# Two conv-FFN up-projections as Strassen block products inside a two-block transformer kernel

## The chip, the cores and the metric

One core of one Trainium2 chip runs the whole kernel in one launch. The metric is device time in microseconds (us). Engines are named as in the profile: PE is TensorE (PEld its weight loads), DVE VectorE, ACT ScalarE, POOL GpSimd, SP SyncE, which issues weight loads from DRAM.

## What is computed

Two transformer blocks follow each other on 1024 tokens of 1024 channels (the second adds 16 meta tokens). Each ends with a projection of the mixer's output, a residual with two norms, and a convolutional feed-forward part. In both blocks this tail is, cut to what matters here:

```python
y = mixed @ w_out                                  # 1024 x 1024
x = x + gate * rmsnorm(y)                          # gate is 1 in the second block
h = modulate(rmsnorm(x))                           # no shift in the second block
u = dwconv(h @ w_up, conv) + bias                  # w_up: 1024 x 5632, three taps over tokens
val, g = split(u)                                  # 2816 each
out = (val * silu(g)) @ w_down                     # gelu in the second block
x = x + gate2 * rmsnorm(out)
```

All is float32. A product of float32 matrices is made of three matmuls of rounded parts: high weights on high data, low weights on high data, high weights on low data.

## The kernel before

Data lie transposed: channels on the 128 partitions, tokens along the free axis. `mixer_out_to_ffn` (L3223) builds, for either block, the instruction streams of all five engines from w_out to the gate product; `both_mixers` (L3635) strings the first block's, its down-projection (`DownToMerge`, L2405, which goes on with the second block's input projections), the second block's and its down-projection (`DownToOutput`, L2979) together on each engine.

The streams go by steps. Steps 0 to 15 are w_out: two parts of the tokens (448 and 576 in the first block, 460 and 580 in the second), eight tiles of 128 output channels each. The steps after are up tiles of 128 of the 5632 channels; tile j belongs to pair j // 2, the gate tile when j is even and the value tile when it is odd, 22 pairs. The first FIRST = 11 tiles are done on part 0 of the tokens first and on part 1 later (L3241), the other 33 at once. One step is 8 groups of 128 input channels, for each group three matmuls per piece of columns (L3376 to L3378): 512 columns in the first block (`PIECES1`), 342 in the second.

- SP loads a step's weights, 512 KB, into one of two raw buffers (L3291), once their last user's low part is done.
- ACT rounds them to the high part one step ahead (`weight_high`, L3267), waits for the step's matmuls, copies PSUM to a row buffer (L3453, L3459), multiplies by the middle tap and adds the bias (L3467, the centring), and applies silu or gelu to the gate tile (L3472).
- DVE subtracts the high part from the raw weights (`weight_low`, L3277), adds the two outer taps (L3576) and forms the gate product into `g` in SBUF (L3581), 22 rows of 1024 tokens.
- While PE works at the next steps, the norms of a part run in a chain of eight steps (`chain_of`, L3246): squares, means, a spread of the reciprocals by matmul (L3333), residual (L3499, L3504), stores of x by POOL, second norm, scaling (L3511), rounding to `h_hi` and `h_lo`. The sums of squares are matmuls of one column (L3316, L3323) put between the step's own. Part 1's chain ends before step 27, where the first tile needs it.

The down-projection (`Down`, L2114) takes the tokens in four parts of 256; each of its steps is one of the 22 rows of `g` and one 512 KB weight tile, in three buffers. ACT and DVE split the weights and the 256 columns of `g` two steps ahead (L2201, L2215), PE runs 24 matmuls of 256 columns (L2351 to L2353). Norms and residual of the last part run beside it; POOL loads their x rows (L2329). The rows y, x and the squares of a part lie in `g` itself, in columns that are done with (L2146).

## Time and profile before

| | us |
|---|---|
| median of 3 runs | 3636.86 (3633.42 to 3645.36) |
| profiled execution, from its first to its last instruction (its span) | 3639.3 |
| PE busy in it | 3469.9 |
| DVE busy | 2010.0 |
| ACT busy | 1552.9 |
| POOL busy | 140.0 |

The profile is of one execution on the chip. No time is given for what lies around its span; the span is 0.07% above the median and inside the runs' own range, so it is read as that execution's time. Busy times are of instructions on the engine; matmuls are pipelined, each shown longer than the distance to the next, so PE's rate is read from where tiles start, not from durations. The granted TensorE clock is full over most of the span (mean 0.973).

### The profile page before, as it was taken

The numbers are of one execution on the slowest core, as the hardware profiler recorded it, in microseconds if no ns is written. First come the engines' busy times: TensorE is split into PE (matmuls) and PEld (weight loads), VectorE is DVE, ScalarE is ACT, GpSimd is POOL, SyncE is SP. The second block draws the span as 40 slices with busy tenths as digits, with TensorE's granted clock in tenths as the row PEclk, the third lists the DMA queues.
The fourth block names the chain that finished last, engine by engine and source line by source line (L and its number), as shares of the span: only waits on it lengthen the run. The fifth ranks groups of instructions, "written<-read, shape, count | busy, mean of one in ns | idle before, by whom it ended". The sixth has DMA issues, their size and how long they took to land.

```text
span 3639.3 us, 71215 instructions
## 1 busy us (share of the span) xinstructions
PE 3469.9 (95%) x30719; PEld 3187.7 (88%) x30719; DVE 2010.0 (55%) x3131; ACT 1552.9 (43%) x2539; POOL 140.0 (4%) x267
## 2 busy tenths in 40 slices
PE   7999899999889979999999999999999999999999
PEld 4787779888877878888888999899999899999999
DVE  5477767787757745543335785232224653333676
ACT  4556654444337734433334654111114443333554
POOL 2000000000000001000000111000001000000000
PEclk9999999999989989999999999999999999999999
DMA  6233443223233124211113665111114421111665
GB/s 243 75 129 130 147 171 104 90 82 115 76 70 71 26 80 133 89 58 47 47 47 121 209 215 161 30 33 44 47 47 125 131 71 47 47 47 54 200 214 165
DMA packets 321840, 367.30 MB, mean 101 GB/s; under 512 B 14803, under 2 KB 261046, under 8 KB 321528
## 3 DMA queue, kind: packets, MB, share of 16 engines
q1 hardware_dynamic: 304424, 309.64, 27.3%
q0 software_dynamic: 17104, 53.11, 4.4%
q8 instruction: 243, 3.98, 0.4%
q14 instruction: 69, 0.57, 0.0%
HBM read 302.79 MB, written 59.90 MB: 100 GB/s over the span
## 4 chain that ended last, share of the span: by engine, by line
PE 57%; DVE 3%; ACT 2%; issue 1%; DVEq 0%; DMA 0%; POOL 0%; ACTq 0%
PE psum L3376 10%; PE psum L3378 10%; PE psum L3377 10%; PE psum L2351 4%; PE psum L2826 4%; PE psum L2827 4%; PE psum L2828 4%; PE psum L2353 4%; PE psum L2352 4%; PE psum L2688 1%; DVE u_val L3576 1%; DVE w_lo L3277 1%; PE psum L3323 1%; ACT u_val L3467 0%; DVE g L3581 0%
## 5 line engine op out<-in xcount | busy, mean ns | idle before, releaser
L3376 PE MATMUL psum<-mix_h_hi,w_hi 128*128 128x342 f32 (+5 forms) x1848 | 636.3, 344 | 17.1 <-DVE w_lo L3277 15.2
L3377 PE MATMUL psum<-mix_h_hi,w_lo 128*128 128x342 f32 (+5 forms) x1848 | 632.3, 342 | 0.0
L3378 PE MATMUL psum<-mix_h_lo,w_hi 128*128 128x342 f32 (+5 forms) x1848 | 631.9, 342 | 0.0
L2218 DVE TENSOR_TENSOR w_lo<-w_raw,w_hi 128x1024 fp32r<-128x1024 f32 (+1 forms) x167 | 195.9, 1173 | 398.4 <-ACT w_hi L2208 396.9
L3376 PEld LDWEIGHTS psum<-mix_h_hi,w_hi 128*128 128x128 f32 x1848 | 349.0, 189 | 47.5 <-DVE w_lo L3277 18.6
L2208 ACT ACTIVATE w_hi<-w_raw 128x1024 fp32r<-128x1024 f32 (+1 forms) x167 | 170.3, 1020 | 491.3 <-PE psum L2828 325.3
L3378 PEld LDWEIGHTS psum<-mix_h_lo,w_hi 128*128 128x128 f32 x1848 | 348.9, 189 | 26.8
L3377 PEld LDWEIGHTS psum<-mix_h_hi,w_lo 128*128 128x128 f32 x1848 | 349.2, 189 | 26.3
L3453 ACT ACTIVATE xs<-psum 128x1024 f32<-128x1024 f32 (+1 forms) x66 | 67.9, 1029 | 486.2 <-PE psum L3378 486.2
L2351 PE MATMUL psum<-down_ghi,w_hi 128*128 128x256 f32 x944 | 269.8, 286 | 0.6 <-DVE down_glo L2223 0.3
L2353 PE MATMUL psum<-down_glo,w_hi 128*128 128x256 f32 x944 | 266.9, 283 | 0.0
L2352 PE MATMUL psum<-down_ghi,w_lo 128*128 128x256 f32 x944 | 266.9, 283 | 0.0
L3277 DVE TENSOR_TENSOR w_lo<-w_raw,w_hi 128x1024 fp32r<-128x1024 f32 x142 | 173.4, 1221 | 154.7 <-ACT w_hi L3273 154.4
L2826 PE MATMUL psum<-h_hi,w_hi 128*128 128x348 f32 (+2 forms) x736 | 238.3, 324 | 0.5 <-DVE h_lo L2515 0.5
L2827 PE MATMUL psum<-h_hi,w_lo 128*128 128x348 f32 (+2 forms) x736 | 237.2, 322 | 0.0
L2828 PE MATMUL psum<-h_lo,w_hi 128*128 128x348 f32 (+2 forms) x736 | 236.9, 322 | 0.0
L3576 DVE SCALAR_TENSOR_TENSOR u_val<-xs,prm,u_val 128x1024 f32<-128x1024 f32 x68 | 87.4, 1285 | 247.8 <-ACT u_val L3467 245.3
L757 PE MATMUL psum<-h_hi,w_hi 128*128 128x512 f32 (+1 forms) x536 | 209.0, 390 | 0.7 <-DVE w_lo L923 0.7
L758 PE MATMUL psum<-h_hi,w_lo 128*128 128x512 f32 (+1 forms) x536 | 199.6, 372 | 0.0
L759 PE MATMUL psum<-h_lo,w_hi 128*128 128x512 f32 (+1 forms) x536 | 199.4, 372 | 0.0
L3576 DVE SCALAR_TENSOR_TENSOR u_gate<-xs,prm,u_gate 128x1024 f32<-128x1024 f32 x64 | 82.2, 1285 | 200.1 <-ACT u_gate L3467 197.7
L2351 PEld LDWEIGHTS psum<-down_ghi,w_hi 128*128 128x128 f32 x944 | 180.3, 191 | 1.9 <-DVE down_glo L2223 1.6
(490 smaller groups left out, 7999.1 us busy)
## 6 DMA issues: line engine op xcount, KB each, us to landing
w_raw<-in_w_down SPq DMA_DIRECT2D x118, 512.0 KB, 4.1
w_raw<-in_w_up SPq DMA_DIRECT2D x110, 512.0 KB, 3.7
w_raw<-in_w_in SPq DMA_DIRECT2D x59, 512.0 KB, 4.0
down_w_raw<-in_w_down SPq DMA_DIRECT2D x58, 512.0 KB, 3.9
rw_operands<-step_set SPq DMA_DIRECT2D x16, 1024.0 KB, 6.3
mod_w<-in_w_mod POOLq DMA_DIRECT2D x32, 512.0 KB, 6.1
w_raw<-in_w_out SPq DMA_DIRECT2D x32, 512.0 KB, 3.6
unit<-rw_operands SPq DMA_DIRECT2D x22, 512.0 KB, 5.0
```

The lines of the kernel that those rows point to most:

```text
L757: mm(out, k.w_hi[:, s, w], k.h_hi[:, kk, x], start=(kk == 0), stop=False)
L2351: nc.tensor.matmul(out, w_hi[:, w], g_hi[:, :], start=(n == 0 and c % 2 == 0), stop=False, skip_group_check=True)
L2352: nc.tensor.matmul(out, w_lo[:, w], g_hi[:, :], start=False, stop=False, skip_group_check=True)
L2353: last = nc.tensor.matmul(out, w_hi[:, w], g_lo[:, :], start=False, stop=(n == KF - 1), skip_group_check=True)
L2826: nc.tensor.matmul(out, w_hi[:, w], x_hi[:, xk, x], start=(kk == 0), stop=False)
L2827: nc.tensor.matmul(out, w_lo[:, w], x_hi[:, xk, x], start=False, stop=False)
L2828: last = nc.tensor.matmul(out, w_hi[:, w], x_lo[:, xk, x], start=False, stop=end)
L3277: nc.vector.tensor_tensor(k.w_lo[:, slot(i), :], k.w_raw[:, slot(i), :], k.w_hi[:, slot(i), :].bitcast(F32), ALU.subtract).then_inc(w_low, 1)
L3376: nc.tensor.matmul(out, k.w_hi[:, s, w], xh[:, kk, x], start=(kk == 0), stop=False)
L3377: nc.tensor.matmul(out, k.w_lo[:, s, w], xh[:, kk, x], start=False, stop=False)
L3378: last = nc.tensor.matmul(out, k.w_hi[:, s, w], xl[:, kk, x], start=False, stop=(kk == KD - 1))
L3576: last = nc.vector.scalar_tensor_tensor(out=u[:, :], in0=x[:, left + q:left + q + SEQ], scalar=tap[q], in1=u[:, :], op0=ALU.mult, op1=ALU.add)
```

## The change

An up pair becomes one 2 x 2 x 2 block product in the Strassen-Winograd form. Its blocks: of the weights, value (row 1) and gate (row 2) tiles, each in two halves of 4 x 128 input channels; of h, the same two halves of channels and two halves of the tokens. The seven products are called P1 to P7; P1 and P2 need only half 0 of the tokens. Four operands are sums of blocks of h (`t1` to `t4`, made once, with `b22` copied), four are sums of weight blocks (made for each pair). Each product is 4 groups of three matmuls on n columns: n is 512 in the first block, 516 (two banks of 258) in the second, where 1032 tokens from the 8th on are taken.

The step list (`plan_steps`): 32 half steps of w_out on halves of 512 (516) tokens; 16 early steps, P1 and P2 of the pairs 3, 5, 7, 9, 0, 1, 11, 13; then the late steps of pairs 0 to 21, P6, P7, P5, P4, P3 for the early pairs and P1, P6, P7, P5, P2, P4, P3 for the others. From pair 1 to 14 early and fresh pairs alternate. The weights of a step are split three steps ahead into a ring of four buffers, raw tiles lie in four. P1 is copied by ACT to the value row before P2 is added to it; the other five products are taken by DVE (`take`), with adds and subtracts that put the output rows together. The gate product goes to DRAM, `Down` reads it back in parts of 256 columns through POOL's queue. Chains take sixteen half steps. The core of the diff:

```diff
-FIRST = 11
+EARLY = [3, 5, 7, 9, 0, 1, 11, 13]
...
-    jobs = [(j, (0,)) for j in range(FIRST)] + [(j, (1,)) for j in range(FIRST)] + \
-           [(j, (0, 1)) for j in range(FIRST, TILES_UP)]
+def plan_steps(banks):
+
+    steps = [("O", u, h) for u in range(2 * KD) for h in range(2)]
+    if banks == 1:
+        early = [("P1", EARLY[0])]
+        for last, i in zip(EARLY, EARLY[1:]):
+            early += [("P1", i), ("P2", last)]
+        early.append(("P2", EARLY[-1]))
+    else:
+        early = [(kind, i) for i in EARLY for kind in ("P1", "P2")]
+    late = [(kind, i) for i in range(KF)
+            for kind in (("P6", "P7", "P5", "P4", "P3") if i in EARLY else ("P1", "P6", "P7", "P5", "P2", "P4", "P3"))]
+    return steps + early + late
...
+    def weight_low(dve, s):
+        src, r = source(s)
+        dve.wait_ge(*w_high.at(s + 1))
+        nc.vector.tensor_tensor(ring[s % 4][:, 1, :], src, ring[s % 4][:, 0, :].bitcast(F32), ALU.subtract).then_inc(w_low.sem, 1)
+        if s + 1 < STEPS and s + 1 >= first_late:
+            kind, i = steps[s + 1]
+            if kind == "P6":
+                add_weights(dve, i)
+            elif kind == "P4":
...
+    def add_weights(dve, i):
...
+        dve.drain()
+        nc.vector.tensor_tensor(tmp[0][:, :], g[:, 0:512], g[:, 512:1024], ALU.add).then_inc(w_added.sem, 1)
+        dve.drain()
+        nc.vector.tensor_tensor(g[:, 0:512], g[:, 0:512], v[:, 0:512], ALU.add).then_inc(w_added.sem, 1)
+        nc.vector.tensor_tensor(tmp[1][:, :], tmp[0][:, :], v[:, 0:512], ALU.add).then_inc(w_added.sem, 1)
...
     def gpsimd(pool):
...
+        for m in range(KF):
+            pool.wait_ge(*g_ready.at(m + 1))
+            pool.dma_start(k.g_dram[m], uv[:, :]).then_inc(g_stored.sem, 16)
+            if m >= FIRST_ROWS:
+                pool.wait_ge(*g_stored.at(16 * m))
+                after.load_first(pool, 0 if m == FIRST_ROWS else m - 1, m)
...
     def tensor(pe):
...
+            elif kind == "P4":
+                pe.wait_ge(*took.at(5 * i + 2))
+            elif kind == "P3":
+                pe.wait_ge(*took.at(5 * i + 3))
...
+        for s in range(STEPS):
+            kind, i = steps[s][0:2]
+            pe.wait_ge(*w_low.at(s + 1))
+            bank_free(s)
...
     def scalar(act):
...
+        def centre_gate(i):
+            act.wait_ge(*took.at(5 * i + 4))
...
+        def centre_val(i):
+            act.wait_ge(*took.at(5 * i + 5))
...
+        for s in range(STEPS):
+            kind, i = steps[s][0:2]
+            if s + 3 < STEPS:
+                weight_high(act, s + 3)
...
+            if s >= first_late and i and s == late_at[i]:
+                activate(i - 1)
+            if kind == "O":
+                if steps[s][2]:
+                    act.wait_ge(*acc_done.at(s + 1))
+                    keep_unit(i)
+            elif kind == "P1":
+                keep_p1(s)
+            elif kind == "P2":
+                keep_c11(s)
+            elif kind == "P4":
+                centre_gate(i)
+            elif kind == "P3":
+                centre_val(i)
...
     def vector(dve):
...
+        def add_turns(kk):
...
+            tt(f["t1"], h0[0][kk][:, :].bitcast(F32), b12, ALU.subtract)
+            tt(f["t3"], b12, b22_row, ALU.subtract)
+            dve.drain()
+            tt(f["t1"], f["t1"], h0[1][kk][:, :].bitcast(F32), ALU.add)
+            dve.drain()
+            tt(f["t2"], b22_row, f["t1"], ALU.add).then_inc(t_added.sem, 1)
+            dve.drain()
+            tt(f["t4"], h0[0][kk + 4][:, :].bitcast(F32), f["t2"], ALU.subtract)
+            dve.drain()
+            tt(f["t4"], f["t4"], h0[1][kk + 4][:, :].bitcast(F32), ALU.add).then_inc(t4_added.sem, 1)
...
+            elif e == 14:
+                scale_rows(a, 4)
+                if a == 0:
+                    low_rows(0)
+                else:
+                    add_turns(0)
+            elif e == 15:
+                if a == 0:
+                    low_rows(4)
+                else:
+                    for kk in range(1, 4):
+                        add_turns(kk)
+                    for which in TURNS[0:3]:
+                        low_turns(which)
...
+            if at == 1 and i:
+                val_tap(i - 1, 2)
+            elif at == 2 and i:
+                product(i - 1)
+            if s + 3 < STEPS:
+                weight_low(dve, s + 3)
+            elif s + 3 < STEPS + 2:
+                after.split(dve, s + 3 - STEPS)
+            if at == 0 and i:
+                val_tap(i - 1, 0)
+            elif kind == "P3":
+                gate_taps(i)
...
+            if s in (first_late, first_late + 1):
+                low_turns(TURNS[3 + s - first_late])
+            if s >= first_late:
+                take(s)
...
+    def load_part(self, pool, p):
+        pool.dma_start(self.g_part[p % 2][:, :, :],
+                       self.k.g_dram[:, :, self.cols(p)].rearrange("n p c -> p n c")).then_inc(self.part_landed[p], 16)
...
         for p in range(SEQ // PART):
             pool.wait_ge(self.low, KF * (p + 1))
+            if p + 2 < SEQ // PART:
+                self.load_part(pool, p + 2)
             for kk in range(4):
                 self.load_x(pool, p, kk)
```

`take` waits for the step's matmuls (`acc_done`) and counts `took`, five a pair in the order P6, P7, P5, P4, P3; `at` is the number of steps since the pair's first late one.

## Rows read from the trace of the kernel before

**Rows 1.** The page: busy shares by engine, and the chain that ended last

```profile
PE 3469.9 (95%) x30719; PEld 3187.7 (88%) x30719; DVE 2010.0 (55%) x3131; ACT 1552.9 (43%) x2539; POOL 140.0 (4%) x267
...
PE psum L3376 10%; PE psum L3378 10%; PE psum L3377 10%; PE psum L2351 4%; PE psum L2826 4%; PE psum L2827 4%; PE psum L2828 4%; PE psum L2353 4%; PE psum L2352 4%; PE psum L2688 1%; DVE u_val L3576 1%; DVE w_lo L3277 1%; PE psum L3323 1%; ACT u_val L3467 0%; DVE g L3581 0%
```

**Rows 2.** Timeline of PE: start us, us, engine line op out<-in xcount [idle <-releaser]

```profile
1312.71 0.74 PE L3376 MATMUL psum<-mix_hi,w_hi 128*128 128x448 f32 x1 [11.88 <-DVE w_lo L3277]
...
1949.78 0.28 PE L2351 MATMUL psum<-down_ghi,w_hi 128*128 128x256 f32 x1
...
2734.47 0.37 PE L3376 MATMUL psum<-mix_hi,w_hi 128*128 128x460 f32 x1
...
3361.84 0.28 PE L2351 MATMUL psum<-down_ghi,w_hi 128*128 128x256 f32 x1
```

**Rows 3.** Timeline of ACT, up tiles of the first, then of the second block

```profile
1603.84 1.25 ACT L3467 ACTIVATE u_gate<-xs,prm 128x1024 f32<-128x1024 f32 x1
1605.00 1.05 ACT L3273 ACTIVATE w_hi<-w_raw 128x1024 fp32r<-128x1024 f32 x1
...
1615.04 1.24 ACT L3467 ACTIVATE u_val<-xs,prm 128x1024 f32<-128x1024 f32 x1
...
3327.94 1.03 ACT L3453 ACTIVATE xs<-psum 128x1026 f32<-128x1026 f32 x1 [7.16 <-PE psum L3378]
...
3339.31 1.03 ACT L3453 ACTIVATE xs<-psum 128x1026 f32<-128x1026 f32 x1 [8.11 <-PE psum L3378]
```

**Rows 4.** Timeline of ACT, first block, w_out units of half 0 and half 1

```profile
1324.68 0.55 ACT L3437 ACTIVATE mix_y<-psum 128x448 f32<-128x448 f32 x1 [2.93 <-PE psum L3378]
...
1329.54 0.55 ACT L3437 ACTIVATE mix_y<-psum 128x448 f32<-128x448 f32 x1 [2.92 <-PE psum L3378]
...
1382.25 0.71 ACT L3437 ACTIVATE mix_y<-psum 128x288 f32<-128x288 f32 x2 [0.90 <-PE psum L3378]
...
1390.54 0.71 ACT L3437 ACTIVATE mix_y<-psum 128x288 f32<-128x288 f32 x2 [0.89 <-PE psum L3378]
```

**Rows 5.** Groups by shape on DVE from 1290 us: xcount | busy, mean ns | idle

```profile
L3576 DVE SCALAR_TENSOR_TENSOR u_val<-xs,prm,u_val 128x1024 f32<-128x1024 f32 x68 | 87.4, 1285 | 247.8 <-ACT u_val L3467 245.3
...
L2218 DVE TENSOR_TENSOR w_lo<-w_raw,w_hi 128x512 fp32r<-128x512 f32 x16 | 11.1, 692 | 143.6 <-ACT w_hi L2208 143.6
...
L3499 DVE TENSOR_TENSOR mix_temp<-mix_y,psum 128x576 f32<-128x576 f32 x8 | 5.7, 748 | 0.5 <-PE psum L3337 0.5
```

**Rows 6.** Timeline of DVE, first block, an up tile

```profile
1593.99 2.65 DVE L3576 SCALAR_TENSOR_TENSOR u_val<-xs,prm,u_val 128x1024 f32<-128x1024 f32 x2 [8.88 <-ACT u_val L3467]
1596.71 1.23 DVE L3581 TENSOR_TENSOR g<-u_val,mix_up 128x1024 f32<-128x1024 f32 x1
1597.85 1.22 DVE L3277 TENSOR_TENSOR w_lo<-w_raw,w_hi 128x1024 fp32r<-128x1024 f32 x1
```

**Rows 7.** Groups by shape on ACT from 1290 us

```profile
L2208 ACT ACTIVATE w_hi<-w_raw 128x512 fp32r<-128x512 f32 x16 | 10.1, 632 | 156.7 <-PE psum L2828 156.7
```

**Rows 8.** Timeline of PE, start of the first block's down

```profile
1959.19 0.58 PE L2351 MATMUL psum<-down_ghi,down_w_hi 128*128 128x256 f32 x1 [3.29 <-DVE down_glo L2223]
1959.57 0.41 PE L2352 MATMUL psum<-down_ghi,down_w_lo 128*128 128x256 f32 x1
1959.78 0.41 PE L2353 MATMUL psum<-down_glo,down_w_hi 128*128 128x256 f32 x1
...
1962.12 0.28 PE L2352 MATMUL psum<-down_ghi,down_w_lo 128*128 128x256 f32 x1
1962.24 0.28 PE L2353 MATMUL psum<-down_glo,down_w_hi 128*128 128x256 f32 x1
```

**Rows 9.** A stretch of the first down, and DMA issues: xcount, KB, us to landing

```profile
core 0: us, PE busy (x) PEld busy (x) DVE busy (x) ACT busy (x) POOL busy (x), PEclk, DMA share, GB/s
2000.00:2200.00 200.00, 199.41 (x1674) 198.15 (x1673) 162.79 (x301) 118.30 (x214) 25.79 (x48) 1.00 0.65 211
...
mod_w<-in_w_mod POOLq DMA_DIRECT2D x32, 512.0 KB, 6.1
```

More of the change, by code:

```diff
@@ L2183, in nth @@
     def nth(self, i):
-        return i // 3 + 1 if i < self.TWO else self.TWO // 3 + (i - self.TWO) // 2 + 1
+        return sum(self.slot(j) == self.slot(i) for j in range(i + 1))
     def depth(self, i):
@@ L2917, in vector @@
             elif i + 2 == self.total:
-                self.next.weight_low(dve, 0)
+                for s in range(2):
+                    self.next.weight_low(dve, s)
             if q == 7:
@@ L3206, in vector @@
             self.finish_rows(dve, self.last, half)
-FIRST = 11
+EARLY = [3, 5, 7, 9, 0, 1, 11, 13]
+QUEUE = len(EARLY)
+KEPT = {i: j for j, i in enumerate(EARLY + [i for i in range(KF) if i not in EARLY])}
+X_BUFFER = [6, 7] + [i // 2 - 1 if i % 2 and i < 14 else 6 + i % 2 for i in range(2, KF)]
+FIRST_ROWS = 14
 def half_groups(n):
@@ new lines, in mixer_out_to_ffn @@
+    squared, added, resid, squared2, added2 = (signal(q, t) for q, t in (
+        ("squared", 2 * KD), ("added", 2 * KD - 2), ("residual", 2 * KD), ("squared_again", 2 * KD), ("added_again", 2 * KD)))
+    summed, meaned, rooted, diags, spread = (signal(q, t) for q, t in (
+        ("summed", 2), ("meaned", 4), ("rooted", 4), ("diags", 4), ("spread", 4)))
+    xin_landed = [signal(f"x_landed{s}", 16 * 4) for s in range(4)]
+    x_stored = [signal(f"x_stored{a}", 16 * KD) for a in range(2)]
+    scaled, shifted, high, low = (signal(q, t) for q, t in (
+        ("scaled", 2 * KD), ("shifted", 2 * KD), ("high", KD), ("low", KD)))
@@ L3284, in sync @@
+    def sync(sp):
+        for r in range(TILES):
+            if r >= 4:
+                sp.wait_ge(*w_low.at(released[r - 4]))
+            elif before and r < 2:
+                sp.wait_ge(before.low, before.total - 1 + r)
             elif before:
-                sp.wait_ge(before.low, before.total - 1 + i)
-            if i < UNITS:
-                src = w_out[:, :, unit(i)[1] * P:unit(i)[1] * P + P]
-            else:
-                c = col(job(i)[0])
+                sp.wait_ge(before.merged, KD)
+            if r < UNITS:
+                src = w_out[:, :, r % KD * P:r % KD * P + P]
+            else:
+                if r < UNITS + QUEUE:
+                    c = (EARLY[r - UNITS] + side[1]) * P
+                else:
+                    i, gate = divmod(r - UNITS - QUEUE, 2)
+                    c = (i + side[0 if gate else 1]) * P
@@ new lines, in spreads, with chain @@
+            pe.wait_ge(*diags.at(norm(a, second)))
+            for t, m in half_groups(n):
+                if t == 0:
+                    last = nc.tensor.matmul(spread_out[:, 0:4 * P], k.ones[:, :], dg[:, 0:4, :], start=True, stop=True)
+                elif m < P:
+                    last = nc.tensor.matmul(spread_out[:, t * P:t * P + m], k.ones[0:m, :], dg[0:m, t, 0:m],
+                                            start=True, stop=True)
+            last.then_inc(spread.sem, 1)
+        def chain(a, e, kk):
+            if e == 1 and kk == 1:
+                sums(a)
+            elif e == 2 and kk == 3:
+                spreads(a, 0)
+            elif e == 5 and kk in (0, 2):
+                sum_residual(a, kk // 2)
+            elif 6 <= e <= 10 and kk == 1:
+                sum_residual(a, e - 4)
+            elif e == 10 and kk == 3:
+                sum_residual(a, 7)
+            elif e == 12 and kk == 2:
+                spreads(a, 1)
@@ L3473, in scalar @@
+        activate(KF - 1)
         after.scalar(act)
@@ new lines, in scale_rows @@
+        def scale_rows(a, j0):
+            dve.wait_ge(*spread.at(norm(a, 1)))
+            dve.wait_ge(*x_stored[a].at(16 * KD))
+            dve.drain()
+            for j in range(j0, j0 + 4):
+                row = y[a][:, order[a][j], :]
+                if shift is not None:
+                    nc.vector.tensor_tensor(row, row, spread_out[:, 0:n], ALU.mult).then_inc(scaled.sem, 1)
+                else:
+                    nc.vector.scalar_tensor_tensor(out=row, in0=row, scalar=gain_pre(order[a][j]), in1=spread_out[:, 0:n],
+                                                   op0=ALU.mult, op1=ALU.mult).then_inc(scaled.sem, 1)
@@ L3522, in vector, with val_tap, product @@
+        def val_tap(i, q):
+            dve.wait_ge(*centred_v.at(i + 1))
+            last = tap(i, False, q)
+            if q == 2:
+                last.then_inc(tapped_v.sem, 1)
+        def product(i):
+            dve.wait_ge(*activated.at(i + 1))
+            dve.drain()
+            nc.vector.tensor_tensor(uv[:, :], uv[:, :], ug[:, :], ALU.mult).then_inc(g_ready.sem, 1)
         spec["prepare"]()
@@ L3525, in vector @@
         if not before:
-            weight_low(dve, 0)
-        for i in range(STEPS):
-            if before and i < 4:
-                for kk in (2 * i, 2 * i + 1):
-                    before.merged_low(dve, 1, kk)
-            if i + 1 < STEPS and (i or not before):
-                weight_low(dve, i + 1)
-            elif i:
-                after.split(dve, 0)
-            if 1 <= i <= UNITS and (i - 1) % KD:
-                a, n = unit(i - 1)
-                m = hs[a]["n"]
+            for s in range(3):
+                weight_low(dve, s)
```

848 lines of the change are left out of this document (503 added, 345 removed).

## The prediction, made before the changed kernel had run

> **What bounds the kernel now.** I read the page's busy shares first, then the chain that ended last: TensorE (PE) is busy 95% of the span and most of that chain is PE, with the three matmul lines of the function that changes at its head, 10% each [rows 1]. So the up-projections are on the path, and fewer columns through PE is time, as long as PE stays the one that ends last. The timeline of PE gives the two stretches that change: first block, w_out and up, from 1312.7 to the first down matmul at 1949.8, 637 us; second block 2734.5 to 3361.8, 627 us [rows 2]. In the timeline of ScalarE (ACT) one up tile follows the other every 11.20 us (48 matmuls of 512 columns, 0.233 us each) and, in the second block, every 11.37 us (72 of 342, 0.158 us) [rows 3]. In that rhythm VectorE (DVE) has 8.88 us of idle ahead of a tile [rows 6], so before the change neither DVE nor ACT matters.
>
> **What PE saves.** A pair (gate tile and value tile) needs 8 block products before and 7 after, 12 matmuls each. First block: 22 x (22.40 - 7 x 2.80) = 62 us. In the second block a product is 24 matmuls of 258 columns: a 256-column one is 0.12 us after the other [rows 8], so 2.88 us a product, and 22 x (22.73 - 20.16) = 57 us; with the slope between 342 and 512 columns it would be 2.89. Together 119 us.
> The Trainium skill (TensorE: Matmul & The Clock Gate, Back-to-back issue gap) puts isolated matmuls at columns / 2.4 plus 2.5 ns, 216 ns at 512 and 110 ns at 258. By it the change would save another 37 us in the second block; the row at 512 shows 233 instead, so the trace doesn't bear that out, and I take the rows.
>
> **What DVE and ACT get.** Durations for 512 elements: weight split L on DVE 0.69 us [rows 5]; two DVE instructions without a drain between them start 0.08 us before the other's end, with a drain 0.08 after it [rows 6]. So L fills 0.61; a drained sum S, or a product taken from PSUM T (0.75 at 576, so 0.68 at 512 [rows 5]), fills 0.76; a 1024 tap V is 1.285 + 0.08 = 1.36, the gate product R 1.23 + 0.08 = 1.31 [rows 5, 6]. A pair before cost DVE 2 splits of 1024, 4 V, R. Now it has 7 L (5 with its P1 and P2 done early), 4 sums, 5 T, 4 V, R: 17.7 us fresh, 15.7 early, against 19.6 and 14.0 on PE. An early pair alone overruns; an early and a fresh one make 34.2 (one sum more in front of an early pair) against 33.6.
> Then the order within the engines. ACT's step begins with the next weights' high part; the centring (1.15 us from its start to the next instruction's [rows 3]) stands at the end of steps P4 and P3, and waits for DVE's T. DVE's next step begins with L, which waits for that high part, which is queued on ACT behind the centring. So twice per pair DVE stands still for about 0.1 + 1.15 + 0.6 (a 512 high part takes 0.63 [rows 7]) + 0.1 = 1.9 us, with nothing to put there. DVE's list of steps, from one P3 taken to the next (W is the 1.9; of three sums in a row the last fills 0.61). Early pair: P6 W+L+V+T 4.63, P7 V+L+T 2.73, P5 R+L+3S+T 4.81, P4 L+T 1.37, P3 W+L+2V+T 5.99, together 19.5 us. Fresh pair before an early one: P1 W+L+V 3.87, P6 V+L+S+T 3.49, P7 R+L+T 2.68, P5 L+3S+T 3.50, P2 L 0.61, P4 L+T 1.37, P3 W+L+S+2V+T 6.75, together 22.3; fresh before fresh one S less, 21.5. PE can't run away from it: P4 waits for T of P7, P3 for T of P5, and its weights are made three steps ahead. PE's waits are then 8.2 us in an early-fresh couple and 1.9 in a fresh pair.
> Pairs 1 to 21: 7 early x 19.5 + 6 x 22.3 + 8 x 21.5 = 442 us in the first block, 444 in the second (516 elements), against 372 and 383 on PE.
>
> **The entry to the late steps** (counted from PE's start of step 45, the last third but one of the early products). Half 1 of y must be scaled, shifted, turned into four sums of operands and rounded. DVE: scaling and two splits to 8.7; four rows of six drained sums, 4.4 each, to 27.7; three groups of four lows to 35.2; then L, four lows, T to 39.4; L, three weight sums, four lows, T of P7 to 45.4. P6 also waits for the eighth early pair, kept on ACT behind three groups of rounding, 31.8. P4 starts at 45.4, P3 ends at 51.0, where eight steps of 2.80 would end at 22.4: 28.6 us lost, 27.5 in the second block. Before, eleven first-half tiles hid this. T of P3 ends at 55.9; so PE's last P3 ends at 55.9 + 442 - 7.2 (its lead over T) = 491 from step 45; second block 492.
>
> **The rest.** w_out, half 0: 8 x 5.60 + 2.2 for the low clock at the start, as before, 47.0 (before 8 x 4.86 [rows 4]). Half 1: a unit took 8.29 us with two sums of squares between its 48 matmuls of 288 [rows 4], which by the slope from the 256 ones are 0.134 each, 6.4; so 0.95 for one such insertion, and 11 of them make 8 x 5.60 + 10.5 = 55.3 (in the second block five groups of columns for four, 1.06 each). At steps 32 and 33 PE waits for the low rows of half 0 and then for the last square: 6.8 us, plus 3 at a lower clock; 3.4 and 2 in the second block. 13 early steps 36.4 + 10.5 = 46.9. **First block** 47.0 + 55.3 + 9.8 + 46.9 + 491 = 650, before 637: +13. **Second block** 47.2 + 57.8 + 5.4 + 49.1 + 492 = 652, before 627: +25. **Into down**: the first two down steps start at once; the third needs DVE, which ends its last product 7 us behind PE: PE waits 8.5 us where it waits 3.29 now [rows 8]: +5 twice. The gate products now go through DRAM. The store is hidden: 512 KB land in about 6 us [rows 9], and the next centring of the value comes 9.7 us after. Reading back, 2.9 MB a part on POOL's queue and ahead of the residual's x rows, meets weights at 211 GB/s and a DMA share of 0.65 [rows 9]: between 0 and 24 us; there is a third of the engines free, so I take 5. PSUM banks, the three-step weight lead and the four raw tiles cost nothing: their waits lie inside those above (without that cover the tightest is a bank's, P3 waiting for T of P5, 1.7 us in a couple). The halves of 512 + 512 tokens in place of 448 + 576 leave the attention's last copies the same elements in fewer instructions: under 1 us of gain, taken as none.
> Sum: +13 + 25 + 10 + 5 = +53 on the profiled execution's span of 3639.3, which is 2.4 above the median of 3636.9: **3690 us** (3689.9). Its own range, with 3% on DVE's slots (27 us), 0.2 us on each wait (17) and 10 on the entry: 3650 to 3730.
>
> **Rivals.**
> **Faster: DVE's standstill behind ACT doesn't take place**, because the answer is there before L asks. Then couples run at 34.2, fresh pairs at PE's 19.6, and the 133 us of the two late stretches over PE's time shrink to about 10. Entry costs stay. First block 586, second 595, down +5: 3639 - 51 - 32 + 5 = 3561, or 3559 against the median. Between the ends it decides by the length of the standstill: at 1.1 us instead of 1.9 the kernel breaks even. For it: 8.88 us of idle DVE, and engines that in this trace answer each other in 0.1 us. Against: the order in the code is fixed. 24%, with all that lies between.
> **Slower: the part loads hold the weights up.** Six loads of 2.9 MB, each with some 8 weight tiles under way; if the two share evenly a tile lands in over 4 us where PE eats one in 2.87, and after the slack of two tiles PE waits about 4 us a load: +24 on the forecast, 3714. For it: share 0.65. Against: it is not 1.
> The Trainium skill (DMA: Bandwidth & Descriptors, Queues, rings and completion order) says that each DMA engine serves its queues in turn, packet by packet. By that rule the loads take from the weights instead of waiting behind them.
> **Slower: the clock.** After a wait of 3.29 us PE's 256-column matmuls lay 0.21 apart, not 0.12, for nearly 3 us [rows 8], the lower level of 1.2 GHz. The wait before P4 of an early pair is 4.9 us. If four steps of each couple ran there, 33.6 + 11 is 44.8 and PE is slower than DVE: +3 a couple, 40 in all 14 early pairs, 3730. For one or two steps it hides behind DVE.
> These two 14% together. The change does do what it says: 154 steps of 12 matmuls of 512 are 7/8 of the columns.
>
> **How the numbers follow.** DVE-bound with standstill 62%; faster rival 24%; the slower two 14%. About 0.3% (11 us) is what a measurement can tell from no change: 6% for that, taken from the first two cases' edges. Slower 0.70, same 0.06, faster 0.24. The range leaves out the lower part of the fast rival and the far end of the slow ones: 3600 to 3740.
>
> **What would show it.** PE's idle up by about 170 us, its releasers DVE's takes (P7, P5) and w_lo; a gap of some 20 us in PE before the first P6 of each block; DVE near 85% busy in the late stretch, with idle of 1.9 us ended by ACT's w_hi twice a pair; couples 42 us apart, fresh pairs 21.5. Wrong if couples come at 34 us, if DVE's idle there is under 1 us a pair, if PE's waits in down end on DMA, or if the entry gap is short.

## The result and the profile after

The changed kernel takes **3720.8 us** (median of 4 runs, 3717.3 to 3728.6) where the kernel before takes 3639.7 (4 runs): ratio 1.0224, 95% interval 1.0205 to 1.0244. That is slower, by 81 us; forecast were 53. First the page of the profiled execution (its span 3722.4 us): busy times, and the chain that ended last by engine.

```profile
PE 3406.6 (92%) x30711; PEld 3081.6 (83%) x30711; DVE 2404.7 (65%) x3809; ACT 1582.8 (43%) x2735; POOL 182.5 (5%) x335
...
PE 38%; DVE 14%; issue 4%; DVEq 3%; ACT 3%; DMA 2%; ACTq 0%; POOL 0%
...
g_scratch<-mix_u_val POOLq DMA_DIRECT2D x44, 512.0 KB, 4.0
down_g_part<-g_scratch POOLq DMA_DIRECT2D x6, 2816.0 KB, 17.2
```

PE is busy 63 us less than before and yet the span is 83 longer [rows 1]: PE stands idle 316 us instead of 169, and DVE works 395 us more. (The forecast saving for PE was 119 us at full clock. The mean granted clock is 0.957 where it was 0.973, and how much of the difference that makes was not traced.) The timeline of PE, at the starts of the stages:

```profile
1307.49 0.79 PE L3586 MATMUL psum<-mix_hi,mix_w_split 128*128 128x512 f32 x1 [9.67 <-DVE mix_w_split L3407]
...
1495.80 0.77 PE L3586 MATMUL psum<-mix_t_hi,mix_w_split 128*128 128x512 f32 x1 [23.76 <-ACT mix_x_val L3680]
...
1970.42 0.28 PE L2369 MATMUL psum<-down_ghi,down_w_hi 128*128 128x256 f32 x1
...
2763.65 0.28 PE L3586 MATMUL psum<-mix_hi,mix_w_split 128*128 128x258 f32 x1
...
3431.66 0.28 PE L2369 MATMUL psum<-down_ghi,down_w_hi 128*128 128x256 f32 x1
```

| stage, from such starts | before | after | difference | forecast |
|---|---|---|---|---|
| ahead of the first block | 1312.7 | 1307.5 | -5 | 0 |
| first block | 637.1 | 662.9 | +26 | +13 |
| its down and what follows, to the second block | 784.7 | 793.2 | +9 | +7.5 |
| second block | 627.4 | 668.0 | +41 | +25 |
| its down, to the end | 277.4 | 290.8 | +13 | +7.5 |

Each block has the 24 us gap ahead of its first P6. The rest is in the late steps. Here are PE's waits in the changed kernel over the whole run (engine, line, what it waited for: us in total, times, longest):

```profile
PE psum L3586 <- DVE mix_x_gate L3858: 86.2, 34, 5.7
PE psum L3586 <- ACT mix_x_val L3680: 46.3, 2, 23.8
PE psum L3586 <- DVE mix_w_split L3407: 19.4, 29, 9.7
...
PE psum L2369 <- DVE down_glo L2240: 12.2, 6, 5.1
```

L3858 is DVE's take of P7, for which P4 waits. Why DVE is late with it, where it had 8.88 us of idle ahead of a tile before [rows 6], shows in its own timeline, one fresh pair of the first block from one P4 taken to the next:

```profile
1835.21 0.69 DVE L3862 TENSOR_TENSOR mix_x_gate<-mix_u,psum 128x512 f32<-128x512 f32 x1
1837.73 0.69 DVE L3407 TENSOR_TENSOR mix_w_split<-mix_w_raw,mix_w_split 128x512 fp32r<-128x512 f32 x1 [1.83 <-ACT mix_w_split L3402]
1838.52 2.64 DVE L3870 SCALAR_TENSOR_TENSOR mix_u_gate<-mix_x_gate,prm,mix_u_gate 128x1024 f32<-128x1024 f32 x2
1841.25 0.69 DVE L3864 TENSOR_TENSOR mix_x_val<-psum,mix_u 128x512 f32<-128x512 f32 x1
1843.78 0.69 DVE L3407 TENSOR_TENSOR mix_w_split<-mix_w_sum,mix_w_split 128x512 fp32r<-128x512 f32 x1 [1.83 <-ACT mix_w_split L3402]
1844.56 2.64 DVE L3870 SCALAR_TENSOR_TENSOR mix_u_val<-mix_x_val,prm,mix_u_val 128x1024 f32<-128x1024 f32 x2
...
1855.55 0.69 DVE L3426 TENSOR_TENSOR mix_w_sum<-mix_w_sum,mix_w_raw 128x512 f32<-128x512 f32 x1
1856.93 0.69 DVE L3407 TENSOR_TENSOR mix_w_split<-mix_w_sum,mix_w_split 128x512 fp32r<-128x512 f32 x1 [0.70 <-ACT mix_w_split L3402]
1857.71 0.69 DVE L3862 TENSOR_TENSOR mix_x_gate<-mix_u,psum 128x512 f32<-128x512 f32 x1
```

And ACT over the first two of those takes:

```profile
1835.94 1.25 ACT L3687 ACTIVATE mix_u_gate<-mix_x_gate,prm 128x1024 f32<-128x1024 f32 x1 [1.54 <-DVE mix_x_gate L3862]
1837.09 0.61 ACT L3402 ACTIVATE mix_w_split<-mix_w_raw 128x512 fp32r<-128x512 f32 x1
1841.98 1.25 ACT L3696 ACTIVATE mix_u_val<-mix_x_val,prm 128x1024 f32<-128x1024 f32 x1 [4.28 <-DVE mix_x_val L3864]
1843.13 0.61 ACT L3402 ACTIVATE mix_w_split<-mix_w_sum 128x512 fp32r<-128x512 f32 x1
```

DVE takes P4 (ends 1835.90). ACT's centring starts at 1835.94, the next weights' rounding, queued behind it, at 1837.09, and DVE's split at 1837.73: 1.83 us idle, the standstill forecast at 1.9. The same follows the take of P3. A third one, 0.70 us, was not forecast: the last of three weight sums (L3426) has to be rounded by ACT before DVE can split it, and DVE has nothing to do in between.

### The profile page after: what moved, and what is told of

The parts are those of the page before. It is cut to its first block, busy times and chain, and to the rows that moved or that the text cites. A ratio compares the mean times of both kernels' runs of the same rounds, so it can differ in the third digit from the quotient of the medians.

```text
span 3722.4 us, 73022 instructions
## 1 busy us (share of the span) xinstructions
PE 3406.6 (92%) x30711; PEld 3081.6 (83%) x30711; DVE 2404.7 (65%) x3809; ACT 1582.8 (43%) x2735; POOL 182.5 (5%) x335
## 4 chain that ended last, share of the span: by engine, by line
PE 38%; DVE 14%; issue 4%; DVEq 3%; ACT 3%; DMA 2%; ACTq 0%; POOL 0%
PE psum L3586 5%; PE psum L3588 4%; PE psum L3587 4%; PE psum L2846 4%; PE psum L2847 4%; PE psum L2848 4%; PE psum L2369 3%; PE psum L2371 3%; PE psum L2370 3%; DVE mix_u_val L3870 3%; DVE mix_u_gate L3870 2%; DMA down_w_raw<-in_w_down 2%; DVE mix_w_split L3407 2%; ACT mix_w_split L3402 2%; PE psum L2705 1%
## 5 line engine op out<-in xcount | busy, mean ns | idle before, releaser
L2235 DVE TENSOR_TENSOR down_w_lo<-down_w_raw,down_w_hi 128x1024 fp32r<-128x1024 f32 x228 | 270.5, 1186 | 442.2 <-ACT down_w_hi L2209 440.1
L3586 PE MATMUL psum<-mix_t_hi,mix_w_split 128*128 128x258 f32 (+1 forms) x1056 | 358.2, 339 | 145.6 <-DVE mix_x_gate L3858 86.2
L2369 PE MATMUL psum<-down_ghi,down_w_hi 128*128 128x256 f32 x1408 | 404.5, 287 | 12.4 <-DVE down_glo L2240 12.2
L2371 PE MATMUL psum<-down_glo,down_w_hi 128*128 128x256 f32 x1408 | 399.7, 284 | 0.0
L2370 PE MATMUL psum<-down_ghi,down_w_lo 128*128 128x256 f32 x1408 | 399.5, 284 | 0.0
L3586 PEld LDWEIGHTS psum<-mix_t_hi,mix_w_split 128*128 128x128 f32 x1056 | 211.0, 200 | 180.7 <-DVE mix_w_split L3407 106.1
L3587 PE MATMUL psum<-mix_t_hi,mix_w_split 128*128 128x258 f32 (+1 forms) x1056 | 351.2, 333 | 0.0
L3588 PE MATMUL psum<-mix_t_lo,mix_w_split 128*128 128x258 f32 (+1 forms) x1056 | 350.8, 332 | 0.0
L2369 PEld LDWEIGHTS psum<-down_ghi,down_w_hi 128*128 128x128 f32 x1408 | 271.6, 193 | 14.5 <-DVE down_glo L2240 14.1
L2370 PEld LDWEIGHTS psum<-down_ghi,down_w_lo 128*128 128x128 f32 x1408 | 271.8, 193 | 0.3
L2371 PEld LDWEIGHTS psum<-down_glo,down_w_hi 128*128 128x128 f32 x1408 | 271.5, 193 | 0.0
L3587 PEld LDWEIGHTS psum<-mix_t_hi,mix_w_split 128*128 128x128 f32 x1056 | 211.3, 200 | 15.9
## 6 DMA issues: line engine op xcount, KB each, us to landing
down_g_part<-g_scratch POOLq DMA_DIRECT2D x6, 2816.0 KB, 17.2
```

The source lines that it names most:

```text
L2235: last = self.nc.vector.tensor_tensor(self.lo[s][:, 0:w], self.raw[s][:, 0:w], self.hi[s][:, 0:w].bitcast(F32), ALU.subtract)
L2369: nc.tensor.matmul(out, w_hi[:, w], g_hi[:, :], start=(n == 0 and c % 2 == 0), stop=False, skip_group_check=True)
L2370: nc.tensor.matmul(out, w_lo[:, w], g_hi[:, :], start=False, stop=False, skip_group_check=True)
L2371: last = nc.tensor.matmul(out, w_hi[:, w], g_lo[:, :], start=False, stop=(n == KF - 1), skip_group_check=True)
L3586: nc.tensor.matmul(out, w[:, 0, c], xh[:, x], start=(first and kk == 0), stop=False, skip_group_check=True)
L3587: nc.tensor.matmul(out, w[:, 1, c], xh[:, x], start=False, stop=False, skip_group_check=True)
```

## The experiments

All times below are medians beside runs of the kernel before on the same chip. The experiments ran on four chips, on which the kernel before takes 3636.9 to 3644.4 us, so small differences between two of these kernels are better read from their ratios than from their microseconds. The stage times come from one profiled execution of each. "Late steps" are the time from ACT's first to its last centring of a value in a block, a couple is an early and a fresh pair (mean over the first 14 intervals). The last column has the usual distance between the P3s of two fresh pairs at the end of a block, on PE.

| kernel | us | ratio to before (95%) | late steps, 1st / 2nd block | couple | fresh pair |
|---|---|---|---|---|---|
| changed kernel | 3720.8 | 1.0205 to 1.0244 | 454.3 / 454.8 | 42.8 | 22.5 |
| rounding ahead of centring | 3619.6 | 0.9928 to 0.9963 | 401.9 / 404.0 | 37.6 | 19.6 to 20.0 / 20.1 |
| sum order | 3720.6 | 1.0189 to 1.0241 | 447.5 / 448.7 | 42.3 | 21.9 |
| both | 3619.2 | 0.9917 to 0.9964 | 400.5 / 404.0 | 37.6 | 19.6 / 20.1 |
| both, takes first | 3621.7 | 0.9918 to 0.9952 | 403.6 / 404.5 | 37.6 | 20.1 / 20.2 |
| first, sums on GpSimd | 3636.2 | 0.9976 to 0.9995 | 401.5 / 403.2 | 37.8 | 19.6 / 20.1 |

**Is it the standstill?** The rounding for the next step goes ahead of the centring in ACT's queue:

```diff
+            elif kind in ("P4", "P3"):
+                if s + 4 < STEPS:
+                    weight_high(act, s + 4)
+                if kind == "P4":
+                    centre_gate(i)
+                else:
+                    centre_val(i)
```


> On ScalarE the rounding of the weights of the step after the next three stands ahead of the centring in the steps P4 and P3, and nothing else changes. Theory (VectorE stands still behind ScalarE's centring, 1.83 us of idle twice a pair): both idles go, a pair costs VectorE 3.8 us less. A couple of an early and a fresh pair goes from 43.2 to 35.6 us, two fresh pairs lie 19.6 us apart in the first block and 20.2 in the second, where TensorE itself ends last. Late steps 455 us -> 382 and 385; the whole kernel 3721 - 144 = 3577 us. Rival (the standstill only stands in front of other work that is late anyway, a product's release or a drain): VectorE's idle moves to other lines and couples stay above 40 us: 3690 or more. In between, if one of the two standstills was real: about 3650.

The kernel takes 101 us less and is 0.5% faster than the kernel before, from the order of two instructions. Both 1.83 us idles are gone and fresh pairs go at PE's pace. So the theory holds, and the rival with couples above 40 falls. But the expectation was 144 us: couples stop at 37.6 where it had 35.6. In this kernel's DVE timeline the split no longer waits, and a tap does:

```profile
1837.61 0.68 DVE L3407 TENSOR_TENSOR mix_w_split<-mix_w_sum,mix_w_split 128x512 fp32r<-128x512 f32 x1
1839.07 2.65 DVE L3875 SCALAR_TENSOR_TENSOR mix_u_val<-mix_x_val,prm,mix_u_val 128x1024 f32<-128x1024 f32 x2 [0.78 <-ACT mix_u_val L3696]
```

The taps read what ACT centres, and three of a couple's four centrings make DVE wait 0.78 us, 2.3 us a couple. One wait of 0.3 for a rounding is left. DVE's filled time is 34.4 (32.4 busy, 2.0 of short gaps and drains). Together that is 37.1, which three of the first block's seven couples take. The others take 0.3 to 1.6 us more, mostly because DVE waits 0.3 to 1.0 for PE's product, and so the mean is 37.6. So the 3.1 us of waits for centring in the expectation of the GpSimd run below are 0.8 too high.

**The third wait.** The sum that P6 needs is made second:

```diff
-    SUM = {"P5": 1, "P7": 2, "P6": 3, "P3": 4}
+    SUM = {"P5": 1, "P6": 2, "P7": 3, "P3": 4}
```


> Of the three weight sums of a pair the one that P6 needs is made second instead of third; ScalarE rounds it while VectorE makes the last one. Theory: the idle of 0.70 us ahead of P6's weight split, once a pair, falls to about 0.1; VectorE sets the pace, so 42 pairs x 0.6 = 25 us less, 3696 us, with couples at 42.0 and fresh pairs at 21.9 us. Rival (that wait is hidden in front of a later one): 3721, the two standstills behind the centring grow by what this one gives.

Fresh pairs come down to the 21.9 expected, couples only by 0.4, the late steps by 7 and 6 us: half of what was expected. In couples that wait is 0.4 us in the changed kernel, not 0.7. The median shows nothing of it: in this kernel's profile the same code ahead of the first block took 11 us longer (see the last section). So the median is inconclusive, and the timeline shows a term that is real but smaller.

> The edits of the two kernels before together. Theory: couples of 35.6 - 1.2 = 34.4 us, close to TensorE's 33.6, fresh pairs at TensorE's 19.6 and 20.2: another 16 us below the first alone, 3561 us. Rival (the waits are in one chain, so that the second edit gives nothing once the first is made): 3577, no more than the first edit alone.

The time is the same as with the first edit alone: with the two standstills gone PE sets the pace of fresh pairs, and the third wait is covered. The rival is right.

**Order or sum of DVE's work?** What is left in couples is 37.6 against PE's 33.6.

```diff
+            if s >= first_late and s + 4 < STEPS and steps[s + 4][0] == "P6":
+                add_weights(dve, steps[s + 4][1])
+            if at == 0 and i:
+                val_tap(i - 1, 0)
+            elif at == 1 and i:
+                val_tap(i - 1, 2)
+            elif at == 2 and i:
+                product(i - 1)
```


> On top of the two edits together (rounding ahead of centring, sum order; 3619 us): in each step VectorE takes the product before the taps and the gate product of the pair before, and makes the three weight sums behind the take. The early pairs there still take 17.3 us against TensorE's 14.0, with TensorE waiting 1.3 us before P4 for the take of P7 and 1.8 before P3 for that of P5, and VectorE standing 0.79 us before a tap for the centring. Theory (what is left is the order of VectorE's work in the early pairs): couples go from 36.9 to about 34.6 us, 7 couples in each of two blocks, 32 us: 3587 us. Rival (VectorE's sum of work over a couple, not its order, sets 36.9): 3619 us, the waits only move to P3's take.

Early pairs fall from 17.3 to 16.7 us, the fresh ones between them rise from 20.1 to 20.8 in the second block, and the sum stays. The rival is right: a couple is DVE's filled time and its waits for ACT, in whatever order.

**Work taken off DVE.** The four weight sums of a pair go to GpSimd (`nc.gpsimd.tensor_tensor` in place of `nc.vector.tensor_tensor`, in the loop over the gate products, with waits for the splits that read the same buffers).

> On top of the first edit (rounding ahead of centring; 3620 us), the four weight sums of a pair are made by GpSimd instead of VectorE. VectorE is busy 32.3 us of a couple's 37.6 there, with 2.0 of drains and 3.1 us of waits for centring. Theory (VectorE's sum of work sets the couples): 8 sums of 0.76 us less a couple, the couples come down to TensorE's 33.6, 7 x 3.6 us in each of two blocks: 3570 us. Rival (the sums on GpSimd and VectorE's instructions on two operands in SBUF hinder each other, so that one engine's time is added to the other's): VectorE's splits and taps get longer than 0.69 and 1.28 us and the couples stay at 37 us or more: 3620 us or above.

Groups by shape over a stretch of the first block's late steps, of the kernel with both edits first (1570 to 1900 us), then of this one on DVE (1590 to 1916 us), then its sums on GpSimd over the whole run (xcount | busy, mean ns):

```profile
L3875 DVE SCALAR_TENSOR_TENSOR mix_u_gate<-mix_x_gate,prm,mix_u_gate 128x1024 f32<-128x1024 f32 x34 | 43.7, 1285 | 10.6 <-ACT mix_u_gate L3687 8.9
L3407 DVE TENSOR_TENSOR mix_w_split<-mix_w_raw,mix_w_split 128x512 fp32r<-128x512 f32 x59 | 40.5, 686 | 1.3 <-ACT mix_w_split L3402 1.3
...
L3869 DVE TENSOR_TENSOR mix_x_val<-psum,mix_u 128x512 f32<-128x512 f32 x17 | 11.8, 693 | 1.6
```

```profile
L3884 DVE SCALAR_TENSOR_TENSOR mix_u_gate<-mix_x_gate,prm,mix_u_gate 128x1024 f32<-128x1024 f32 x34 | 55.3, 1626 | 10.7 <-ACT mix_u_gate L3696 8.6 <-issue 0.4
L3407 DVE TENSOR_TENSOR mix_w_split<-mix_w_raw,mix_w_split 128x512 fp32r<-128x512 f32 x58 | 50.8, 876 | 1.8 <-ACT mix_w_split L3402 1.8
...
L3878 DVE TENSOR_TENSOR mix_x_val<-psum,mix_u 128x512 f32<-128x512 f32 x17 | 11.8, 693 | 1.6
```

```profile
L3417 POOL TENSOR_TENSOR mix_w_raw<-mix_w_raw,mix_w_raw 128x512 f32<-128x512 f32 x44 | 88.3, 2007 | 17.0 <-issue 17.0
...
L3420 POOL TENSOR_TENSOR mix_w_sum<-mix_w_sum,mix_w_raw 128x512 f32<-128x512 f32 x44 | 57.3, 1302 | 271.8 <-DVE mix_w_split L3407 271.8
```

The rival is right. A sum costs GpSimd 1.30 us on one line and 2.01 on another, which runs beside DVE's taps for 63 of its 88 us. The gate tile's taps on DVE go from 1285 to 1626 ns, the splits of raw weights from 686 to 876. Within this one run, taps that no GpSimd sum overlaps keep 1285 ns, and such splits 685. The take, which reads one operand from PSUM, stays at 693, beside a sum or not. So DVE, relieved of 8 sums of 0.76 us a couple, is busy only some 1.1 us less (31.2 for 32.3), and it waits more, among others for ACT's rounding of the slower sums. Couples stay at 37.8. The first P6 of the two blocks starts 6 and 10 us later after step 45, and by the ratios (0.9985 for 0.9946) the kernel is 14 us slower than its base. The Trainium skill (SBUF — State Buffer, Who interferes with whom) says that a DVE instruction with two SBUF inputs contends with a GpSimd one that reads SBUF, and that one with at most one SBUF input, outside the two-port modes, does not. The rows agree in both halves.

**The entry.** First, on the changed kernel, the chain of norms of each half alone was laid two steps earlier (two residual rows a step, second norm at the ninth step of the chain instead of the eleventh).

> The changed kernel with one part edited: in each half's chain the residual is made two rows a step from the third of its steps on, so that the second norm, the scaling, the rounding and the turned operands begin two steps earlier. Theory (the entry to the late steps waits for VectorE's own work behind the last norm, some 45 us of it, and steps 32 and 33 wait for half 0's low rows): both begin two steps sooner. The gap of 26 us ahead of the first P6 shrinks by 6 to 7 us in each block, and the waits at steps 32 and 33 (6.6 and 2.4 us in the first block, 1.9 and 4.8 in the second) by some 6 and 3: 3721 - 22 = 3699 us. Rival (the chain is paced by the x rows and ScalarE, not by the steps it is laid on): the same waits appear inside the chain's steps: 3721 us.

It takes 3718.6 us (ratio 1.0177 to 1.0219, where the changed kernel has 1.0205 to 1.0244): by the ratios 9 us less, within the intervals, where 22 were expected. In the profiles the blocks are 1 and 3.5 us shorter. The timeline of PE says where the rest went:

```profile
1495.69 0.76 PE L3584 MATMUL psum<-mix_h,mix_w_split 128*128 128x512 f32 x1 [23.29 <-ACT mix_x_val L3673]
```

The same gap, now ahead of the last early product (`mix_h`), not of P6 (`mix_t_hi`): ACT's keeping of the early product's PSUM stands in its queue behind the roundings of the turned operands, which wait for DVE's sums. So the next kernel, on top of the chain and of both edits, moved those roundings behind ACT's last keep (its copy out of PSUM), and made the sums in stages with fewer drains, all in one run:

```diff
             elif kind == "P2":
                 keep_c11(s)
+                if s == first_late - 1:
+                    for which in TURNS[0:3]:
+                        round_turns(which)
```


> On top of the two edits together (3619 us), the entry to the late steps: the chain of the halves two steps earlier, the sums of the turned operands made row by row in stages without a drain between rows, with the last sum of t4 behind the first three lows, and ScalarE's roundings of the turned operands behind its last keep of an early product instead of ahead of three of them. In the run with the chain alone the gap had only moved one step forward (28.0 us at step 47 in place of 29.2 at step 48), since ScalarE's keep stood behind the roundings, which wait for VectorE. Theory (ScalarE's queue turns VectorE's 18 us of sums into TensorE's wait): the gap before the first P6 shrinks from 26 to 6-8 us, about 5 us come back before P4: 15 us a block, 3588 us. Rival (VectorE's own work up to P4, 45 us behind the last norm, is the bound): the wait moves from P6 to P4, 3 to 5 us a block from the drains alone: 3611 us.

It takes 3598.1 us, 0.9861 to 0.9894 of before, 21 below its base (23 by the ratios) and between the two expectations. Its PE timeline over the first entry:

```profile
1475.18 0.77 PE L3584 MATMUL psum<-mix_h,mix_w_split 128*128 128x512 f32 x1 [3.71 <-ACT mix_x_val L3670]
1490.75 0.77 PE L3584 MATMUL psum<-mix_t_hi,mix_w_split 128*128 128x512 f32 x1 [11.14 <-DVE mix_t_lo L3824]
1509.79 0.76 PE L3584 MATMUL psum<-mix_t_hi,mix_w_split 128*128 128x512 f32 x1 [8.33 <-DVE mix_x_gate L3869]
```

The 23.8 us halve, and 8.3 come back before P4: from step 45 on P4 starts only 2.8 and 4.6 us sooner, as the rival had it (3 to 5). In the profiles the first block gained 1 us, the second 10. Two things stand against calling the place of the roundings the cause of the 21. The profiled execution is the slowest of this kernel's four runs (3607.4, the others 3595.4 to 3598.7), and that of its base the fastest of its four (3611.6, the others 3618.8 to 3624.7), so the profiles do not hold most of the gain. And the kernel with all edits (below), which has the chain and takes first but leaves the roundings where they were, has blocks just as short in its profile: 605.1 and 610.1 us for 607.2 and 610.9 here, where the base has 607.9 and 620.5. Which of this run's edits gains how much stays open.

**Into down.** The third down step's split on DVE ahead of the last pair's taps:

> The changed kernel with one part edited: VectorE splits the third down step's weights and gate rows ahead of the last pair's value taps and product, not behind them. Theory (the wait of 5.1 and 5.0 us before the third down step is VectorE's last 4.6 us of taps and product with their wait for the centring): both waits go, and with them the lower clock behind them, 10 to 16 us: 3708 us. Rival (the split waits for ScalarE or the gate rows' own landing): under 2 us of gain, 3720.

It takes 3728.4 us (1.0217 to 1.0246) and is not faster than the changed kernel. PE's timeline has 3.13 us ahead of the third step in place of 5.10, and then

```profile
1996.73 1.03 PE L2588 MATMUL psum<-ident,meta_rows 16*128 16x16 f32 x8 [6.17 <-DMA meta_rows<-in_meta_tokens]
```

where the changed kernel waits 3.12. GpSimd's timeline in the changed kernel:

```profile
1980.13 0.53 POOL L3466 DMA_DIRECT2D g_scratch<-mix_u_val  x1 [15.56 <-DVE mix_u_val L3888]
...
1983.41 0.55 POOL L2223 DMA_DIRECT2D down_g_part<-g_scratch  x1 [2.21 <-DMA g_scratch<-mix_u_val]
1983.95 0.52 POOL L2760 DMA_DIRECT2D meta_rows<-in_meta_tokens  x1
```

The meta load stands behind the last gate product, its store and its landing; with the split first that product is later still. So it was moved ahead of them, in the kernel with both edits, with the split moved too:

> On top of the two edits together (3619 us), the way into down: the third down step's split ahead of the last taps on VectorE, and on GpSimd's queue the meta tokens' load ahead of the last gate product's store. In the run with the split alone TensorE's wait for VectorE fell from 5.1 to 3.1 us while that for the meta rows rose from 3.1 to 6.2. Theory (the meta load stands in GpSimd's queue behind the last gate product, its store and the waiting for it, some 11 us behind the last P3): the wait for the meta rows goes wholly, 5 to 8 us off the first down stage, 2 to 3 off the second: 3610 us. Rival (the meta rows are late because weights and part loads fill the DMA engines): it stays at 3 us or more and the kernel at 3619 us.

It takes 3616.2 us (0.9915 to 0.9943) against 3619.2. The wait for the meta rows is gone, so its cause was the queue, not the DMA engines. The expected gain of 5 to 8 us in the first down stage did not come: PE now waits 2.43 and 2.52 us for DVE's splits, and that stage is 1 us shorter in the profiles.

**The part loads.**

> Leaves out the reading back of the gate products for the third and fourth part of both down stages (one row of 22 is loaded in place of all), so that two of the six loads of 2.9 MB are left; what is multiplied in these parts is old data. Forecast's term (five microseconds for six loads, by contention with the weights): about 3 us less, 3718. Rival (the loads hold the weights up, 4 us each): 16 us less, 3705. If the loads cost nothing: 3721. The wait of 3.1 us of TensorE for the meta tokens' rows stays in each case, since the load ahead of it stays.

It takes 3717.8 us (1.0193 to 1.0237), which is 3 us less and inside the intervals. In the profiles the two down stages are 5.0 and 6.8 us shorter than in the changed kernel (but 2.1 and 3.5 shorter than with the sum order, whose down code is the same). The entry's kernel, with all loads, has a second down stage as short as this one (284.2 and 284.0 us), so single stages scatter by as much as two loads cost. What names the loads is the place: 80 to 90 us and some 150 us into both stages PE's matmuls start 0.6 to 2.7 us apart in the kernels with the loads, and not here. In the changed kernel these places add up to some 4 to 5 us a stage. So the loads cost about 2 us each, not the rival's 4.

**Together.** Chain, takes first and split first on top of both edits:

> All edits together on the changed kernel: rounding ahead of centring, the sum order, takes first, the chain two steps earlier, the third down step's split ahead of the last taps. If the theories of all hold and the gains are separate: 3619 - 32 - 22 - 13 = 3552 us, 85 below the kernel before. Rival (they share the same microseconds, since VectorE's work at the entry and in the early pairs is the bound): 3590 us.

It takes 3616.6 us (0.9907 to 0.994), 3 us below both edits alone (7 by the ratios), where 3552 was expected and 3590 by its rival. The edits do not add up. The second block is 10 us shorter in the profiles than with both edits (610.1 for 620.5), but the stretch from the first down stage to the second block is 7 longer (796.3 for 789.4) and the last stage 3. Last, all that had gained, with two more moves at the entry:

> All that gained, together: rounding ahead of centring, the sum order, the entry of the run before (3598 us), the way into down (split first, meta load first), and two more moves at the entry. In the entry's run the gap before P6 had halved, but VectorE reached P4's operands no sooner: it stood 2.2 us twice in the scaling steps, behind ScalarE's shifted rows, and made b22's four lows (2.5 us) ahead of the take of P7 that P4 waits for. Now the second half's rows are scaled in one step, the turned operands follow in the next, and the take stands ahead of the lows. Theory (VectorE's order sets P4's start): P4 begins 2.5 to 7 us sooner in each block, and the way into down gives 2 to 6 us in all: 3598 - 5 to 14 - 2 to 6, that is 3586 us. Rival (VectorE's sum of work at the entry is all there is): 3594 us, from the way into down alone.

It takes 3600.4 us (0.9864 to 0.9906), no better than the entry's 3598.1, and above both expectations (3586 and 3594). P4 starts 7.1 and 2.4 us sooner after step 45, as the theory has it. In the profiles the blocks are 7.5 and 4.9 us shorter and the first down stage 4.6, but the second is 6.5 longer and the code ahead of the blocks 5.7. Either version is about 1.2% faster than the kernel before.

## Why the prediction was right or wrong

**PE's saving** was right per pair: with the standstills gone fresh pairs run at 19.6 us in the first block and 20.1 in the second, forecast 19.6 and 20.2.

**The standstill** was right in cause and size: 1.83 us for 1.9, twice a pair, and taking it away gives 101 us back. The prediction's "faster" rival was wrong about this order of instructions, and its estimate of 3559 us for a kernel without the standstill was too low: it takes 3620. About 40 of these 60 us are in the late steps, where it had 10 us over PE's time. The runs show three waits of a tap for the centring, 0.78 each, in a couple, and one of 0.3 for a rounding, which neither case had counted. (Its 133 us over PE's time are 131 by its own figures, 442 + 444 - 372 - 383.)

**The list of DVE's steps** is the term that was mis-sized. Early pairs took 19.8 (forecast 19.5), fresh before early 22.9 (22.3), fresh before fresh 22.5 (21.5). Of that last 1.0 us, 0.78 is the step written as "3S" followed by "L + T" without a wait: the third sum goes through ACT before L. Over a couple DVE's filled time is 35.0 where the list had 34.2; which instruction is longer than its slot was not traced. Together the late steps take 454 and 455 us, forecast 442 and 444: 23 of the 30 us by which the profiled execution is above its forecast. The sign "DVE near 85% busy" was not met either, though its own list of 34.2 filled us in 41.8 gives only 82%. From 1600 to 1800 us DVE is busy 151.64 us of 200, which is 76%:

```profile
core 0: us, PE busy (x) PEld busy (x) DVE busy (x) ACT busy (x) POOL busy (x), PEclk, DMA share, GB/s
1600.00:1800.00 200.00, 170.11 (x669) 132.24 (x668) 151.64 (x195) 67.87 (x94) 4.78 (x9) 0.91 0.25 71
```

**The entry** came out as listed. From PE's start of step 45 the first P3 ends after 52.6 us (51.0), in the second block after 50.5 (50.5). w_out took 46.5 and 54.6 (47.0 and 55.3), in the second block 46.7 and 59.2 (47.2 and 57.8). That P6 waits for ACT's kept early pair was right too (P6 starts at 33.2 and 31.3 for 31.8), and the chain's experiment shows that this queue holds P6's start back by itself.

**Into down** the step failed twice, in opposite directions. PE's wait for DVE ahead of the third down step was put at 8.5 us and is 5.1 (3.29 before [rows 8]), because PE's last P3 ends 3.9 us ahead of the end of DVE's take of it, not 7.2. That PE ends later adds 3.3 us to each block, so this one term accounts for most of what is left of the 30 us. Missing was the meta tokens' load: the change puts gate product stores and their landings into GpSimd's queue ahead of it, and PE waits 3.1. PE's granted clock over the 31.6 us from the first down matmul is 0.84, where it is 0.95 before. The two stages cost 9 and 13 us for 7.5 each. Only the first has the meta load, and what else makes the second longer was not traced.

**The part loads**, 5 us for six, are too low by more than half if each costs about 2, though within what the medians can tell: 2816 KB land in 17.2 us while the down stage's weights of 512 KB land in 4.3. The prediction's rule from the Trainium skill (DMA: Bandwidth & Descriptors, Queues, rings and completion order), that each DMA engine serves its queues in turn, agrees with the small waits of PE that go when the loads go (matmuls 0.6 to 2.7 us apart); no run here shows the turns themselves. The clock as a rival didn't take place: between 1600 and 1800 us the granted clock is 0.91 (row above), and couples still go at DVE's pace.

## What to carry to other kernels

When fewer matmuls move the bound to another engine, write that engine's list with every hand-over in it, and look at what stands ahead of each hand-over in the other engine's queue: here one rounding behind one centring cost 100 us, more than the blocks lost. Moving a step forward gains little while another in-order queue (ACT's keeps behind its roundings, GpSimd's load behind its stores) still holds the release. GpSimd was no help to DVE here for sums of two SBUF tensors, since DVE itself works on such pairs. And when a kernel bundles several edits, its gain names none of them.

## What the runs showed that was not expected

The code ahead of the first block is the same in the changed kernel and all 12 experiments, and yet its first matmul starts between 1303.4 and 1318.7 us in their profiles (changed kernel 1307.5, sum order 1318.7, both edits 1303.4), most of it in the stage between the first projection and the attention (554.9 to 569.3 us). Edits of some 10 us are therefore read from the stages they touch, not from the span, and the medians of different kernels have such a spread in them.

Sums of two 128x512 tensors in SBUF took GpSimd at least 1.26 us, 1.8 times DVE's 0.69, and up to 2.27 beside DVE. DVE's instructions on two SBUF tensors got longer by 28% in their mean for splits of raw weights, and by 33% for the value tile's taps (1285 to 1703 ns).
